# Norm, residual and norm weights by token tile between the stages of a two-block transformer, with the next norm's scale as a row on the products

## What is computed

```python
def rms_norm(x, g):
    y = xf * lax.rsqrt(jnp.mean(xf * xf, -1, keepdims=True) + EPS)
    return (y * g).astype(x.dtype)

for i in range(2):                       # first block
    a = rms_norm(h, norm_g[i, 0])
    a = mla_mixer(a, ...) if i == 0 else diff_mixer(a, ...)
    h = h + rms_norm(a, norm_g[i, 1])
    f = conv_ffn(rms_norm(h, norm_g[i, 2]), up, conv_w, conv_b, down)   # hidden 2816, conv over 3 tokens
    h = h + rms_norm(f, norm_g[i, 3])
# second block
h1 = rms_norm(x, g_mix);  x = x + (two attentions, gated, on h1 @ w_in) @ w_out
x = x + hier_moe(rms_norm(x, g_ffn))     # 32 experts, top 2
return rms_norm(x, g_final)
```

## Time and profile before

| | |
|---|---|
| median of 3 runs | 1363.15 us (1363.07 to 1370.86) |
| the profiled execution | 1361.37 us, its span 1359.6 us, mean granted clock 0.992 |
| PE, DVE, ACT, POOL busy | 1285.8, 510.5, 549.0, 568.2 us |
| DMA | 341 MB, 251 GB/s over the span, 422 to 430 GB/s in most of the last 13 of 40 slices |
| chain that ended last | PE 72%, DMA 15%, DVE 5%, ACT 4%, POOL 2%, issue 2% |

### The profile page before, as it was taken

How to read it: one execution, slowest core, us unless ns; L and a number is a source line. 1 busy time by engine, 2 the same in 40 slices (tenths; PEclk the granted TensorE clock), 3 DMA queues, 4 the chain that set the end, 5 groups by cost and what they waited for, 6 DMA issues and landing times.

```text
span 1359.6 us, 20047 instructions
## 1 busy us (share of the span) xinstructions
PE 1285.8 (95%) x7971; PEld 958.3 (70%) x7971; DVE 510.5 (38%) x1307; ACT 549.0 (40%) x853; POOL 568.2 (42%) x132
## 2 busy tenths in 40 slices
PE   6999999999998899999999899999999999999996
PEld 5867899998986799999877788854445444454442
DVE  2334544445265454444657264431112111121113
ACT  4544655556477465555544465221111111111112
POOL 5532788885954188888568555400000000000000
PEclk9999999999999999999999899999999999999998
DMA  7622566654633176665446443599999999999994
GB/s 268 216 81 89 154 199 200 190 187 154 217 124 94 62 213 190 186 185 172 154 147 201 135 145 128 208 422 426 429 429 428 428 428 430 429 430 429 429 427 176
DMA packets 154821, 341.22 MB, mean 251 GB/s; under 512 B 8473, under 2 KB 119418, under 8 KB 142202
## 3 DMA queue, kind: packets, MB, share of 16 engines
q1 hardware_dynamic: 154746, 340.18, 67.2%
HBM read 339.10 MB, written 1.05 MB: 250 GB/s over the span
## 4 chain that ended last, share of the span: by engine, by line
PE 72%; DMA 15%; DVE 5%; ACT 4%; POOL 2%; issue 2%; SPq 0%; ACTq 0%; DVEq 0%
PE bank L649 16%; PE bank L651 15%; PE bank L650 15%; DMA ring<-in_w 10%; PE bank L1211 10%; PE bank L1237 5%; DMA xspare<-in_w 4%; PE bank L1163 2%; PE bank L748 2%; POOL parts L611 2%; PE bank L659 1%; ACT parts L1281 1%; PE bank L1193 1%; PE bank L1097 1%; PE bank L782 1%
## 5 line engine op out<-in xcount | busy, mean ns | idle before, releaser
L611 POOL TENSOR_TENSOR parts<-raw,parts 128x2048 fp32r<-128x2048 f32 (+4 forms) x128 | 568.0, 4465 | 305.5 <-ACT parts L1281 305.5
L649 PE MATMUL bank<-xh,parts 128*128 128x256 f32 x1032 | 289.0, 280 | 12.1 <-ACT room L1318 5.9
L650 PE MATMUL bank<-xl,parts 128*128 128x256 f32 x1032 | 286.7, 278 | 0.0
L651 PE MATMUL bank<-xh,parts 128*128 128x256 f32 x1032 | 286.6, 278 | 0.0
L1281 ACT ACTIVATE parts<-raw 128x2048 fp32r<-128x2048 f32 (+4 forms) x128 | 235.9, 1853 | 33.1 <-PE bank L649 18.0
L1211 PE MATMUL bank<-ring,room 128*64 128x512 f32 x768 | 226.2, 594 | 8.6 <-DMA ring<-in_w 5.8
L649 PEld LDWEIGHTS bank<-xh,parts 128*128 128x128 f32 x1032 | 194.5, 189 | 18.9 <-issue 10.6
L650 PEld LDWEIGHTS bank<-xl,parts 128*128 128x128 f32 x1032 | 195.3, 189 | 0.8
L651 PEld LDWEIGHTS bank<-xh,parts 128*128 128x128 f32 x1032 | 194.6, 189 | 0.0
L1211 PEld LDWEIGHTS bank<-ring,room 128*64 128x64 f32 x768 | 73.3, 137 | 112.5 <-issue 112.5
L649 PE MATMUL bank<-parts,xh 128*128 128x512 f32 (+5 forms) x304 | 114.6, 377 | 9.6 <-POOL parts L611 2.8
(11 more groups left out here) (255 smaller groups left out, 1804.4 us busy)
## 6 DMA issues: line engine op xcount, KB each, us to landing
ring<-in_w SPq DMA_DIRECT2D x71, 2048.0 KB, 23.1
raw<-in_ffn_w_up SPq DMA_DIRECT2D x88, 512.0 KB, 4.9
room<-in_w SPq DMA_DIRECT2D x12, 2048.0 KB, 20.1
raw<-in_ffn_w_down SPq DMA_DIRECT2D x44, 512.0 KB, 3.9
xspare<-in_w SPq DMA_DIRECT2D x11, 2048.0 KB, 26.8
raw<-in_w_in SPq DMA_DIRECT2D x40, 512.0 KB, 4.2
raw<-in_diff_w_qkv SPq DMA_DIRECT2D x24, 512.0 KB, 4.5
raw<-in_mla_w_o SPq DMA_DIRECT2D x8, 512.0 KB, 4.6
```

Of the source, the lines that this page charges most:

```text
L611: pool.tensor_tensor(low[:, p % PARTS, 0:n], raw[:, p % RING, 0:n], high[:, p % PARTS, 0:n], ALU.subtract).then_inc(low_ready, 1)
L649: first = pe.matmul(out_, a[0], b[0], start=start, stop=False)
L650: pe.matmul(out_, a[0], b[1], start=False, stop=False)
L651: return first, pe.matmul(out_, a[1], b[0], start=False, stop=stop)
```

## The change

- **By token tile.** `turn_over` replaces `post` and `normed`. For t = 0, then 1: the two output halves times weights, the tile's own sum and scale (`refined` with n=1), half 0 of `h`, half 0 of `xn` = `h` times weights (`tensor_tensor`, no scale). Then half 1 of `h` for both tiles. ACT's `out_sums` guesses after every second bank.
- **POOL.** `gains` multiplies half 1 of `xn` for both tiles, placed in POOL's order behind the low part of the next stage's second piece.
- **The scale as a row at all four.** ACT squares `h` after the high parts (`x_next`), DVE refines, makes `diag`; PE makes the row in a bank of its own after the first FFN piece, or after the first piece of q; ACT copies it to `late_row` (for k also times a constant). In the FFN, DVE multiplies every tile's bank by the row first (`rows_put`), and only then ACT takes the centre tap. The copies of q and k become multiplications on DVE, v's copies take the token's scale.
- **ACT before attention.** The five `split` calls between copies become one `split(W["qkv"] + 7)` behind the row's copy.
- `WAIT` goes from 32 to 8.

```diff
@@ plan
+    groups("row1", 1, [4])
     groups("x2", 4, [0, 1, 2, 3])
     groups("diff_q", 5, [4, 5, 6, 7, 2])
+    groups("row2", 1, [3])
...
@@ gpsimd
+            def gains(site):
+                pool.wait_ge(gpre_here, 16 * (site + 1))
+                for t in range(NT):
+                    pool.wait_ge(h_ready, 2 * (site - 1) + t + 1)
+                    pool.tensor_tensor(xn[:, t, 512:D], h[:, t, 512:D], gpre[:, 512:D], ALU.mult).then_inc(xn_ready, 1)
+            next_stage = {W[name] + 1: n + 1 for n, name in enumerate(["ffn0", "qkv", "ffn1", "qi"])}
+            def low_of(p):
+                lows(p, WIDTH[p])
+                if p in next_stage:
+                    gains(next_stage[p])
...
@@ tensor
-            WAIT = 32
+            WAIT = 8
...
+            def scales_in_rows(n):
+                pe.wait_ge(diag_ready, n)
+                g = G[f"row{n}" if n < 4 else "row"]
+                b = begin(g)
+                for t in range(NT):
+                    ins = pe.matmul(b[:, t * P:t * P + P], cs[:, C_ONE:C_ONE + P], diag[:, t], start=True, stop=True)
...
                 up(b, 0)
+                scales_in_rows(2 * l + 1)
                 up(b + 1, 1)
...
             for n in range(5):
                 two_heads(G["diff_q"] + n, W["qkv"] + n)
+                if n == 0:
+                    scales_in_rows(2)
...
@@ scalar
-                act.wait_ge(sums_ready, outs_done[0])
-                guess(st[:, 16:18], st[:, 18:20], D)
+                    if n % 2:
+                        outs_done[0] += 1
+                        act.wait_ge(sums_ready, outs_done[0])
+                        guess(st[:, 16 + n // 2:17 + n // 2], st[:, 18 + n // 2:19 + n // 2], D)
...
-                act.wait_ge(up_full, 1 + n)
+                act.wait_ge(rows_put, 1 + n)
...
+            def x_next(site):
+                high_tiles(f"x{site}", HALVES, 4)
+                h_sums(site, 28, 8448)
+                if site < 4:
+                    g = G[f"row{site}"]
+                    full(act, g)
+                    if site == 2:
+                        act.activation(late_key_row, bank[BANK[g]][:, 0:S], ACT.Copy, scale=HD_SCALE).then_inc(key_row, 1)
+                    copy(g, late_row, bank[BANK[g]][:, 0:S])
...
-            for x in range(5):
-                split(W["qkv"] + x + 3)
-                two_heads(G["diff_q"] + x, QKV[x])
+            split(W["qkv"] + 7)
...
@@ vector
+                def scale_of(t):
+                    gained(t, 0)
+                    dve.wait_ge(post_squares, 4 * site + 2 * t + 2)
+                    dve.tensor_tensor(st[:, 18 + t:19 + t], st[:, 2 + 2 * t:3 + 2 * t], st[:, 3 + 2 * t:4 + 2 * t],
+                                      ALU.add).then_inc(sums_ready, 1)
+                    gained(t, 1)
+                    dve.wait_ge(sums_ready, 2 * site + t + 1)
+                    refined(st[:, 16 + t:17 + t], st[:, 18 + t:19 + t], n=1)
...
                 for t in range(NT):
+                    scale_of(t)
+                    added(t, 0)
+                    dve.tensor_tensor(xn[:, t, part[0]], h[:, t, part[0]], gpre[:, part[0]], ALU.mult).then_inc(xn_ready, 1)
+                for t in range(NT):
+                    added(t, 1)
+                late_scales(name, site + 1)
...
+                dve.wait_ge(up_full, 1 + n)
+                both = bank[b][:, :].rearrange("p (a s) -> p a s", a=2)
+                dve.tensor_tensor(both, both, late_row.unsqueeze(1).to_broadcast([P, 2, S]), ALU.mult).then_inc(rows_put, 1)
                 dve.wait_ge(centre, 2 * n + 2)
```

More of the change, by code:

```diff
@@ L192, in plan @@
     groups("diff_t3", 1, [2])
-    for name, n in [("x3", 4), ("x4", 4), ("qi", 4), ("row", 1), ("qa", 2), ("qi_t", 2),
+    groups("x3", 4, [4, 5, 6, 7])
+    groups("row3", 1, [4])
+    turn[0] += 4
+    for name, n in [("x4", 4), ("qi", 4), ("row", 1), ("qa", 2), ("qi_t", 2),
                     ("ki_t", 1), ("ka", 2), ("qa_t", 2), ("index", 8), ("va", 2), ("ka_t", 2), ("qb", 2), ("kb", 2),
@@ L998, in _ @@
             by_token(G["qi"], W["qi"], X, [3, 3, 2], [256, 328])
-            pe.wait_ge(diag_ready, 1)
-            b = begin(G["row"])
-            for t in range(NT):
-                ins = pe.matmul(b[:, t * P:t * P + P], cs[:, C_ONE:C_ONE + P], diag[:, t], start=True, stop=True)
-                if t == 0:
-                    behind(ins)
-            end(ins, G["row"])
+            scales_in_rows(4)
             columns("qa")
@@ L1750, in x_gained, with turn_over, gained @@
                 dve.tensor_copy(st[:, 30:32], st[:, 28:30]).then_inc(scales_ready, 1)
-            def post(site, banks, ring_groups):
+                if site:
+                    for t in range(NT):
+                        ins = dve.tensor_scalar(diag[:, t], ident, st[:, 28 + t:29 + t], None, ALU.mult)
+                    ins.then_inc(diag_ready, 1)
+            def turn_over(site, banks, ring_groups, name):
                 dve.wait_ge(gpost_here, 16 * (site + 1))
-                for n, b in enumerate(banks):
-                    t, hf = divmod(n, 2)
+                dve.wait_ge(gpre_here, 16 * (site + 2))
+                part = [slice(512 * hf, 512 * hf + 512) for hf in range(2)]
+                def gained(t, hf):
+                    n = 2 * t + hf
@@ L1765, in post @@
-                dve.wait_ge(sums_ready, site + 1)
-                refined(st[:, 16:18], st[:, 18:20])
-                for g in ring_groups or []:
-                    moved(dve, g)
-                for t in range(NT):
-                    dve.scalar_tensor_tensor(h[:, t, :], xn[:, t, :], st[:, 16 + t:17 + t], h[:, t, :],
-                                             ALU.mult, ALU.add).then_inc(h_ready, 1)
+                    ins = dve.tensor_tensor(xn[:, t, part[hf]], bank[banks[n]][:, :], gpost[:, part[hf]], ALU.mult)
@@ new lines, in gained @@
+                    ins.then_inc(bank_moved[banks[n]] if ring_groups else vec, 1)
+                    if not ring_groups:
+                        steps[0] += 1
+                def scale_of(t):
[6 more added lines that the diff above has]
+                    refined(st[:, 16 + t:17 + t], st[:, 18 + t:19 + t], n=1)
+                    for g in (ring_groups or [])[2 * t:2 * t + 2]:
+                        moved(dve, g)
@@ L1949, in ffn @@
             def ffn(l):
+                moved(dve, G[f"row{2 * l + 1}"])
                 for j in range(6):
@@ L1973, in _, with two_heads @@
             link(dve.tensor_scalar(st[:, 15:16], subT[:, :], 1.0 - LAM_INIT, None, ALU.mult))
+            def two_heads(g, name):
+                full(dve, g)
+                dve.tensor_tensor(view(512 * int(name[1]) + 2048 * (name[0] == "k"), 512).rearrange("p (a s) -> p a s", a=2),
+                                  bank[BANK[g]][:, :].rearrange("p (a s) -> p a s", a=2),
+                                  (late_key_row if name[0] == "k" else late_row).unsqueeze(1).to_broadcast([P, 2, S]),
+                                  ALU.mult).then_inc(bank_moved[BANK[g]], 1)
+            dve.wait_ge(key_row, 1)
+            moved(dve, G["row2"])
+            for x in range(5):
+                two_heads(G["diff_q"] + x, QKV[x])
             def outputs_scaled(m):
```

90 lines of the change are left out of this document (35 added, 55 removed).

## The result

The changed kernel takes 1379.5 us (median of 7 runs, 1375.5 to 1381.7) against 1363.1 us (7 runs, 1360.6 to 1370.9): ratio 1.0115, 95% interval 1.0093 to 1.0137. In a second session it was 1.0148 (1.0124 to 1.0173). The forecast was 1370.0 (+6.8 us) with a range of 1358 to 1378: right in sign, less than half of the measured +16.5 us, and the result lies above the range.

The account below looks back on a forecast made before the run. PE was taken to bound the kernel until weight streaming from 877 us. Terms -1.3 - 1.3 + 2.75 + 1.1 - 0.4 = +0.85, plus 5.95 for the clock, gave +6.8 us: 1370.0 us, range 1358 to 1378.

Parts of the forecast that it names:

- What bounds the kernel: PE before 877 us, then weight streaming of fixed length; PE idle time gained or lost earlier passes one for one.
- The chains: Turnovers: first product 12.2 us after first square at 2 and 4; net -1.3 at 1 and 3, +2.75, +1.1.
- the bound of 0 to +0.6: Turnovers: DVE's last addition to `h` moves at worst into POOL's first half, adding 0 to +0.6 us.
- The wait at the FFN's end: Last tile pair of each FFN: row multiplications do not hide, so PE waits 0.7 us.
- The waits for third pieces: Ahead of each new stage's third weight piece at turnovers 1 to 3: PE waits 3.1 to 3.3 us for POOL's low part.
- PE's row: After the first piece: PE makes the scale's row in 0.45 us, two products and their wait.
- One sentence of this part: Turnover 2, FFN 0's last tile pair: said both banks were free at 304.12 before the change.
- Attention: Differential attention: one of ACT's two late 0.53 us copies, for which PE waited, moves to DVE: -0.4 us.
- The clock: Four turnovers and three third-piece waits: 0 to 1.7 us lost at each, middle 0.85 taken, +5.95 us.
- the full price: 1.7 us lost per place: PE works 3.40 us at clock 0.50 after 3.10 us idle, seen in differential attention.
- Rival 4: Transposes give no clock: all seven places lose the full 1.7 us, 0.85 + 11.9, so 1375.9; chance 0.05.
- Rival 3: FFN tiles bound by the order DVE, ACT, DVE: 1 us lost in 16 pairs or more, 1379 and up; chance 0.07.

Follow-up runs that it names:

- Taking the order back: Heads' scaling ahead of DVE's sixth q/k piece multiplication in differential attention, against the changed kernel with 32 useless products and 12 before each third piece: 1367.6 against 1371.8 us.
- the kernel without the rows: Changed kernel with DVE's multiplication of each FFN bank by the row replaced by a tiny copy; PE's row and its copy stay: 1379.1 us, ratio 1.0126.
- the one with the waits filled: Changed kernel with 32 useless products at the turnovers and 12 more ahead of the third pieces of turnovers 1 to 3: 1371.8 us, ratio 1.0059.
- its repairs: Changed kernel with 32 useless products, the third piece's high part ahead of the row's copy, and attention's heads' scaling before the sixth q/k piece: 1361.3 us, ratio 0.9976.

## Why the prediction was wrong

**What bounds the kernel**: right. A lag gained ahead of 877 us stayed to the end (20.0 us at 748, 20.3 at the end).

**The chains**: nearly right. First product of turnover 1 at 134.72 (forecast 134.2), of turnover 2 12.7 us behind the first square (12.2, and the difference is transposes at the lower clock, with POOL's pair 2.87 against 2.56: its first took 1.64 us while DVE's last addition still ran, its second 1.27, and the bound of 0 to +0.6 for this holds); turnover 4 +1.3 with the FFN's end (forecast 1.1). The wait at the FFN's end 0.72 (0.7). The waits for third pieces 3.09, 3.03 and 3.09 us (3.1, 3.3, 3.1), ended by POOL's low part as told. PE's row took 0.61 us (0.45). Without the clock, the third pieces of turnovers 1 and 3 came 1.8 us earlier (1.3) and that of turnover 2 3.1 later (2.75), transposes at the low clock included. One sentence of this part was false and did no harm: the odd bank was not free at 304.12, PE ended it 5 us later; it was ready before DVE got to it all the same.

**Attention: wrong in sign.** I took off 0.4 us for a copy that leaves ACT and did not ask what is queued behind its replacement on DVE. The result was +1.2 us of wait and 1.3 of clock, 2.5 in the trace. Taking the order back gave 4.2 in time with overlapping intervals, of which the trace shows the 1.3 of wait.

**The clock: the step that failed.** "So 0 to 1.7 us for each of 4 turnovers and 3 waits; both rows are near in kind, and I take the middle" gave 5.95. The trace has 6.7 at the turnovers (1.24, 2.23, 1.35, 1.90) and 4.6 at the third pieces (1.65, 1.45, 1.46): 11.3 over the seven places, 1.6 at each in the mean, near the full price of 1.7, and 2.2 and 1.9 at turnovers 2 and 4, where the low stretch was 10.2 us long in place of 3.4. The second profile has 9.5 over the seven. With attention (1.3) and the hybrid block (1.5) it is 14.1 in the first. Two errors lie in it. A price that the earlier trace rows showed after a wait of 3.10 us was halved because of the earlier trace rows, from which I read that no loss is to be seen. The loss stands there: the 16 transposes took 3.65 us where the same 16 take 2.64 in the earlier trace rows, and the product at 14.20 is not the first behind them but the fourth. The timeline has two slow ones between:

```profile
13.27 0.66 PE L649 MATMUL bank<-parts,xh 128*128 128x384 f32 x1
13.73 0.45 PE L650 MATMUL bank<-parts,xh 128*128 128x384 f32 x1
```

And the top of the bound was one low stretch for each place, where the low clock stood for 10.2 us at turnovers 2 and 4. The rule of the Trainium skill ("TensorE: Matmul & The Clock Gate", "Part 4: PE-mode transpose"), that transposes don't count as busy time like other products, agrees with the traces: with 8 useless products the clock fell in both kernels though 16 transposes ran, and with 32 it stayed. No run tells transposes from mere idle time, so it isn't shown. Rival 4, worked out from the full price at the seven places, gave 1375.9 and had a chance of 0.05; it came within 3.6 us of the result, without a term for attention or the hybrid block. (Rival 3 named the very time, 1379 and up, but for a cause that the kernel without the rows rules out.) Not that every gap is sure to cost: two waits that cost in one kernel did not in another (1.92 us in the kernel before, 2.87 us in the one with the waits filled). But with the earlier trace rows read rightly no row spoke for the halving.

**The product spacing** is what the first profile had beyond this. It was no step of the prediction and is no effect of the change: in the second profile of the changed kernel it was absent and the span 1375.0 us.

The hybrid block's 1.5 us is open: a low-clock stretch at 765.5, near one of the kernel before at 761.5 to 768.3, comes and goes from profile to profile.

## What to carry to other kernels

Where a turnover is filled with useless products, they are part of its time: before a shorter chain is worth anything, ask whether each new gap of PE (between groups of transposes, ahead of the next weight piece) still has something in it, and price a gap at a whole low-clock stretch, not at a part of one. Ask as well what the useless products hold up: where they end last, a shorter chain behind them brings nothing. When an operation moves to another engine, read what stands behind it in that engine's order, not only what it frees. And work that an idle engine could do during the turnover (the third piece's high part) was worth as much as the whole reordering with its repairs: two calls of `split` in the kernel before gave 0.24%.

## What the runs showed of the hardware

**Two spacings of the same products.** Within an FFN, products of 128x256 follow one another at 0.113 us or at 0.118, for a whole stage, with a granted clock of 1.00 and no wait in either. PE in the second FFN of the changed kernel, first profile, and of the one with 32 useless products:

```profile
547.84 0.28 PE L671 MATMUL bank<-xh,parts 128*128 128x256 f32 x1
547.96 0.28 PE L672 MATMUL bank<-xl,parts 128*128 128x256 f32 x1
548.08 0.28 PE L673 MATMUL bank<-xh,parts 128*128 128x256 f32 x1
```

```profile
547.75 0.28 PE L671 MATMUL bank<-xh,parts 128*128 128x256 f32 x1
547.86 0.28 PE L672 MATMUL bank<-xl,parts 128*128 128x256 f32 x1
547.98 0.28 PE L673 MATMUL bank<-xh,parts 128*128 128x256 f32 x1
```

Two spacings are 0.24 us in the first and 0.23 in the second; the mean over the stage is 0.1178 against 0.1136 us, and over the stage it is 4 us. The same kernel had either in its two profiles, another had it in its first FFN, and in the kernel before it stands between 330 and 360 us. It held for a stage; what chooses it no run shows. It may be part of why runs of one kernel lie 5 to 10 us apart, which wasn't tested, and it is why one profile of a kernel was not enough here.

**The low clock comes after the gap.** In the kernel with the waits filled, 12 useless products of 2.91 us, with 0.42 us of idle time behind them, kept the clock at 1.00 where a wait of 3.09 us left empty had 0.51 behind it. But idle time of one length can go either way: 1.92 us had 1.00 behind it in the kernel before and 0.51 with 8 useless products, though the wait was the same.
